# Third block's mixing: projection columns split in three equal banks, feature sums made as rows, last sums moved between halves of the output projection

## What is computed

```python
h = concatenate([meta, x], axis=1)              # 16 meta tokens ahead of 1024 tokens
u = rmsnorm_3(h, norm_mix_g)
x_lru, g_lru, v_cc, g_cc = split(u @ w_in)      # 4 x 512 features
xc = causal_depthwise_conv_3(x_lru, lru_conv_w, lru_conv_b)            # 4 taps
y_lru = rg_lru(xc, ...) * gelu(g_lru)           # gates, then a scan over the tokens
c = causal_depthwise_conv_3(v_cc * sigmoid(g_cc), cc_conv_w, cc_conv_b)  # 31 taps
y_cc = silu(layernorm_3(c, cc_ln_g, cc_ln_b))
y = concatenate([rmsnorm_3(y_lru, out_norm_lru_g), rmsnorm_3(y_cc, out_norm_cc_g)])
h = h + y @ w_out
h = h + square(relu(rmsnorm_3(h, norm_mlp_g) @ w_mlp_up)) @ w_mlp_down
return rmsnorm_3(h, norm_final_g)[:, 16:]
```

## Time and profile before

| | us |
|---|---|
| median of 3 runs (3903.34 to 3906.10) | 3903.86 |
| the profiled execution | 3905.99 |
| its span in the trace | 3904.1 |
| from the first full projection of the third block to the last matmul of out_3b (in the trace) | 2720.3 to 3142.2 |

### The profile page before, as it was taken

How to read it: one execution, slowest core, us unless ns; L and a number is a source line. 1 busy time by engine, 2 the same in 40 slices (tenths; PEclk the granted TensorE clock), 3 DMA queues, 4 the chain that set the end, 5 groups by cost and what they waited for, 6 DMA issues and landing times.

```text
span 3904.1 us, 38123 instructions
## 1 busy us (share of the span) xinstructions
PE 3515.0 (90%) x15786; PEld 2801.9 (72%) x15786; DVE 1294.2 (33%) x1735; ACT 714.9 (18%) x1060; POOL 1205.7 (31%) x1052
## 2 busy tenths in 40 slices
PE   5958997779969999999899999994989979999997
PEld 4556765668847568787688888883777768888886
DVE  4154065022140440313311111125888252222223
ACT  2210144121121440101100000003323220000011
POOL 3201201315423023343334343431432234343431
PEclk9978998889979899999999999997987989999998
DMA  2100100101221001112111111111001001111111
GB/s 113 43 17 27 43 1 22 54 11 54 86 92 52 14 23 44 54 43 86 36 51 44 53 43 54 43 54 60 33 22 65 33 33 53 45 51 45 44 53 43
DMA packets 31638, 179.52 MB, mean 46 GB/s; under 512 B 3744, under 2 KB 4768, under 8 KB 14624
## 3 DMA queue, kind: packets, MB, share of 16 engines
q1 hardware_dynamic: 18864, 137.37, 10.2%
q10 hardware_dynamic: 12656, 40.42, 2.8%
HBM read 163.10 MB, written 14.68 MB: 46 GB/s over the span
## 4 chain that ended last, share of the span: by engine, by line
PE 84%; DVE 11%; ACT 3%; issue 2%; POOL 1%; DMA 0%; DVEq 0%; ACTq 0%; POOLq 0%
PE ps L374 45%; PE ps L403 15%; PE ps L429 4%; PE ps L1635 4%; PE ps L678 2%; PE ps L1726 1%; DVE xlo L335 1%; PE ps L1684 1%; PE ps L1298 1%; DVE c_out L2014 1%; PE ps L1314 1%; PE ps L297 1%; DVE n_sq L329 1%; PE ps L291 1%; PE ps L740 1%
## 5 line engine op out<-in xcount | busy, mean ns | idle before, releaser
L469 POOL TENSOR_TENSOR whi<-raw,par 128x512 fp32r<-128x512 f32 x131 | 145.8, 1113 | 2592.5 <-PE ps L374 1869.5
L473 POOL TENSOR_TENSOR wlo<-raw,whi 128x512 fp32r<-128x512 f32 x524 | 783.6, 1496 | 41.7
L374 PE MATMUL ps<-xhi,whi 128*128 128x512 f32 x2304 | 723.7, 396 | 52.0 <-DVE xlo L335 32.4
L374 PE MATMUL ps<-xlo,whi 128*128 128x512 f32 x2304 | 715.7, 392 | 0.0
L374 PE MATMUL ps<-xhi,wlo 128*128 128x512 f32 x2304 | 714.9, 392 | 0.0
L374 PEld LDWEIGHTS ps<-xhi,whi 128*128 128x128 f32 x2304 | 434.5, 190 | 160.8 <-issue 32.5
L374 PEld LDWEIGHTS ps<-xlo,whi 128*128 128x128 f32 x2304 | 437.0, 190 | 92.4
L374 PEld LDWEIGHTS ps<-xhi,wlo 128*128 128x128 f32 x2304 | 435.8, 189 | 91.9
L471 POOL CAST whi<-raw 128x512 fp32r<-128x512 f32 x393 | 297.8, 758 | 0.0
L1190 DVE TENSOR_TENSOR h<-h,ps 128x1024 f32<-128x1024 f32 x112 | 132.2, 1218 | 414.0 <-PE ps L403 414.0
L403 PE MATMUL ps<-hidden_lo,whi 128*128 128x512 f32 x864 | 269.2, 393 | 0.0
(11 more groups left out here) (423 smaller groups left out, 4170.6 us busy)
## 6 DMA issues: line engine op xcount, KB each, us to landing
raw<-stream SPq DMA_DIRECT2D x131, 1024.0 KB, 4.8
h_scr<-h ACTq DMA_DIRECT2D x2, 4096.0 KB, 12.2
x_in<-xT ACTq DMA_DIRECT2D x4, 1024.0 KB, 14.4
x_again<-xT ACTq DMA_DIRECT2D x4, 1024.0 KB, 8.7
h<-h_scr ACTq DMA_DIRECT2D x1, 4096.0 KB, 13.9
outT<-h ACTq DMA_DIRECT2D x8, 512.0 KB, 3.0
bias<-bias ACTq DMA_DIRECT2D x1, 2560.0 KB, 19.3
o_scr<-o_staged ACTq DMA_DIRECT2D x2, 1024.0 KB, 4.8
```

Source lines behind the costliest of these rows:

```text
L374: mm = nc.tensor.matmul(ps[:, c0 + c:c0 + c + width], w, x(k, a, width), start=(n == 0 and m == 0), stop=(n == len(ks) - 1 and m == 2))
L469: nc.gpsimd.tensor_tensor(WHI[:, r, t], RAW[:, r, t], one, ALU.mult).then_inc(hi_done, 1)
L473: ins = nc.gpsimd.tensor_tensor(WLO[:, r, t], RAW[:, r, t], WHI[:, r, t].bitcast(F32), ALU.subtract)
```

## The change

1. The meta columns stand ahead of the tokens in `XH3` and `XL3`, so that the 1040 columns are one run. The twelve outputs v, g and x pass them in three pieces of 348, 346 and 346 columns (`THIRDS`), a PSUM bank each. ScalarE's two copies are of 348 columns and of the other two banks (692).
2. Feature sums: the column of ones is the weight and the data moves (`row_sums`), 2 matmuls of 512 columns for 128x1024 elements. The sums come as a row on partition 0 (and 32, for the convolution output). ScalarE takes the root of a row, or copies the rows, into `ROWS3`, and PE turns a row into 8 columns (`columns`, 8 transposes), which VectorE then reads from PSUM.
3. Order: cc_sums 0 and 1 stand ahead of the columns and the spread of the recurrence's norm, cc_sums 2 between the two. cc_sums 3 stands behind half 2 (before: half 4), its columns within half 3 and the two spreads within half 4. `rms_columns` stands before the third tile of out_3b's output 1, the spread before output 2. ScalarE's `keep_half` and `square` calls follow this.

```diff
+            ROWS3 = at("rows_3", A + 83264, [64, T])
+            THIRDS = ((0, 348), (348, 346), (694, 346))
...
-            chunks = ((0, HALF), (HALF, HALF)) if name in ("g_0", "g_2") else ((0, HALF), (HALF, HALF), (T, META))
+
+            chunks = ((META, HALF), (META + HALF, HALF)) if name in ("g_0", "g_2") else THIRDS
             for k in range(KB):
                 if ready:
                     pe.wait_ge(*ready(k))
                 w_hi, w_lo = WHI[:, r, KB * o + k, :], WLO[:, r, KB * o + k, :]
                 for m, (w, x) in enumerate(((w_hi, x3hi), (w_hi, x3lo), (w_lo, x3hi))):
-                    for a, width in chunks:
-                        mm = nc.tensor.matmul(ps[:, c0 + a:c0 + a + width], w, x(k, a, width),
+                    for i, (a, width) in enumerate(chunks):
+                        mm = nc.tensor.matmul(ps[:, c0 + BANK * i:c0 + BANK * i + width], w, x(k, a, width),
                                               start=(k == 0 and m == 0), stop=(k == KB - 1 and m == 2))
-                        if o == k == m == a == 0 and slot > 0:
+                        if o == k == m == i == 0 and slot > 0:
...
-            def column_sums(x, c, first, end):
-
-                for j in range(NT):
-                    mm = nc.tensor.matmul(ps[:, c + j:c + j + 1], x[:, P * j:P * (j + 1)], par("ones", 0, 1),
-                                          start=first and j == 0, stop=end and j == NT - 1)
-                return mm
-
-            def squares(s, c, first):
+            def row_sums(s, c, b, *more):
+
                 pe.wait_ge(*L("m_sq", s + 1))
-                column_sums(SQ3[:, s % 2, :], c, first, s % 4 == 3).then_inc(S("m_sum"), 1)
+                for a in range(0, T, HALF):
+                    for row, x in ((0, SQ3[:, s % 2, :]),) + more:
+                        mm = nc.tensor.matmul(ps[row:row + 1, c + a:c + a + HALF], par("ones", 0, 1), x[:, a:a + HALF],
+                                              start=(b == 0), stop=(b == 3))
+                mm.then_inc(S("m_sum"), 1)
 
             def cc_sums(b):
                 pe.wait_ge(S("cc_conv"), (CCK - 1) * (b + 1))
-                column_sums(CCO[:, b, :], OTHER + 2 * BANK, b == 0, False)
-                squares(4 + b, OTHER + 2 * BANK + NT, False)
+                row_sums(4 + b, OTHER + 2 * BANK, b, (32, CCO[:, b, :]))
+
+            def columns(row, c):
+                for j in range(NT):
+                    mm = nc.tensor.transpose(ps[:, c + j:c + j + 1], ROWS3[row:row + 1, P * j:P * (j + 1)],
+                                             IDENT[row:row + 1, row:row + 1])
+                return mm
...
             for b in range(4):
-                squares(b, OTHER + 3 * BANK, b == 0)
+                row_sums(b, OTHER, b)
+            cc_sums(0)
+            cc_sums(1)
+            pe.wait_ge(*L("l_root", 1))
+            columns(0, OTHER).then_inc(S("l_cols"), 1)
+            cc_sums(2)
             pe.wait_ge(*L("l_diag", 1))
             spread(DIAG3, OTHER).then_inc(S("l_inv"), 1)
-            for b in range(3):
-                cc_sums(b)
 
...
+            def cc_columns():
+                pe.wait_ge(*L("cc_rows", 2))
+                columns(32, OTHER)
+                columns(0, OTHER + BANK).then_inc(S("cc_cols"), 1)
+
+            def cc_spreads():
+                pe.wait_ge(*L("cc_diag", 2))
+                spread(DIAG3, OTHER).then_inc(S("cc_spread"), 1)
+                spread(DIAG3M, OTHER + 2 * BANK).then_inc(S("cc_spread"), 1)
+
+            for o in range(3):
                 lru_half(o)
             cc_sums(3)
-            lru_half(5)
-            pe.wait_ge(*L("cc_diag", 2))
-            spread(DIAG3, OTHER).then_inc(S("cc_spread"), 1)
-            spread(DIAG3M, OTHER + 2 * BANK).then_inc(S("cc_spread"), 1)
-            lru_half(6)
-            lru_half(7)
+            lru_half(3, (2, cc_columns))
+            lru_half(4, (1, cc_spreads))
+            for o in range(5, 8):
+                lru_half(o)
             pe.wait_ge(*L("lh_kept", 8))
...
-                    squares(8 + b, OTHER + 2 * BANK, b == 0)
+                    row_sums(8 + b, OTHER, b)
+
+            def rms_columns():
+                pe.wait_ge(*L("cc_rroot", 1))
+                columns(0, OTHER + 2 * BANK).then_inc(S("r_cols"), 1)
 
             def rms_spread():
                 pe.wait_ge(*L("cc_rdiag", 1))
-                spread(DIAG3, OTHER).then_inc(S("cc_inv"), 1)
+                spread(DIAG3, OTHER + 2 * BANK).then_inc(S("cc_inv"), 1)
 
             feature_tiles(pe, WH["out_3b"], 8, range(4, 8), xhi, xlo, ready=lambda n: L("cc_lo", n + 1),
-                          before={(1, 0): rms_sums, (1, 3): rms_spread, (2, 0): lambda: pe.wait_ge(*L("cc_inv_kept", 1))})
+                          before={(1, 0): rms_sums, (1, 2): rms_columns, (2, 0): rms_spread, (3, 0): lambda: pe.wait_ge(*L("cc_inv_kept", 1))})
...
-                nc.scalar.activation(dst[:, pad + META:pad + LW], trio(q), func).then_inc(free(q), 1)
-                nc.scalar.activation(dst[:, pad:pad + META], trio(q, T, META), func).then_inc(free(q), 1)
+                c, w, rest = 3 * BANK * (q % 2), THIRDS[0][1], THIRDS[1][1]
+                nc.scalar.activation(dst[:, pad:pad + w], ps[:, c:c + w], func).then_inc(free(q), 1)
+                nc.scalar.activation(dst[:, pad + w:pad + LW].rearrange("p (i t) -> p i t", i=2),
+                                     ps[:, c + BANK:c + 3 * BANK].rearrange("p (i t) -> p i t", i=2)[:, :, 0:rest], func)\
+                    .then_inc(free(q), 1)
...
-            nc.scalar.activation(LCOL[:, :], ps[:, OTHER + 3 * BANK:OTHER + 3 * BANK + NT], ACT.Sqrt, bias=EPSC,
-                                 scale=1.0 / (4 * P)).then_inc(S("l_root"), 1)
+            nc.scalar.activation(ROWS3[0:1, :], ps[0:1, OTHER:OTHER + T], ACT.Sqrt, bias=EPSC[0:1, :], scale=1.0 / (4 * P))\
+                .then_inc(S("l_root"), 1)
...
+            for o in range(2):
                 keep_half(o)
             act.wait_ge(S("cc_conv"), 4 * (CCK - 1))
             square(7, CCO[:, 3, :])
+            keep_half(2)
+            act.wait_ge(*L("m_sum", 8))
+            for row in (32, 0):
+                nc.scalar.activation(ROWS3[row:row + 1, :], ps[row:row + 1, OTHER + 2 * BANK:OTHER + 2 * BANK + T], ACT.Copy)\
+                    .then_inc(S("cc_rows"), 1)
             act.wait_ge(*L("cc_var", 4))
             nc.scalar.activation(RCOL[:, :], VCOL[:, :], ACT.Sqrt, bias=EPSC).then_inc(S("cc_root"), 1)
-            keep_half(5)
+            keep_half(3)
+            keep_half(4)
             for b in range(4):
                 act.wait_ge(*L("cc_moved", 2 * (b + 1)))
                 nc.scalar.activation(CCO[:, b, :], CCO[:, b, :], ACT.Silu, bias=par("cc_ln_b_3", b),
@@ -1924,15 +1957,15 @@
                 act.wait_ge(S("cc_silu"), b + 1)
                 nc.scalar.activation(XHI[:, 4 + b, :], CCO[:, b, :], ACT.Copy, scale=par("out_norm_cc_g_3", b))\
                     .then_inc(S("cc_hi"), 1)
-                if b < 2:
-                    keep_half(6 + b)
+                if b < 3:
+                    keep_half(5 + b)
...
-            dve.wait_ge(*L("l_root", 1))
-            v.step(nc.vector.reciprocal(LCOL[:, :], LCOL[:, :]))
+            dve.wait_ge(*L("l_cols", 1))
+            v.step(nc.vector.reciprocal(LCOL[:, :], ps[:, OTHER:OTHER + NT]))
...
-            s1, s2 = (ps[:, OTHER + 2 * BANK + NT * n:OTHER + 2 * BANK + NT * (n + 1)] for n in range(2))
-            dve.wait_ge(*L("m_sum", 8))
+            s1, s2 = (ps[:, OTHER + BANK * n:OTHER + BANK * n + NT] for n in range(2))
+            dve.wait_ge(*L("cc_cols", 1))```

PE, first projection output of the block (v0), before and after. `xhi3` and `xlo3` are the high and low parts of the normed input, `whi` and `wlo` those of the weights:

```order
L1635 MATMUL ps<-xhi3_291,whi_50 128x512 x2
L1635 MATMUL ps<-xhi3_291,whi_50 128x16
L1635 MATMUL ps<-xlo3_292,whi_50 128x512 x2
L1635 MATMUL ps<-xlo3_292,whi_50 128x16
L1635 MATMUL ps<-xhi3_291,wlo_51 128x512 x2
L1635 MATMUL ps<-xhi3_291,wlo_51 128x16
```

24 lines of the change are left out of this document (13 added, 11 removed).

## The result

| | before | after |
|---|---|---|
| median of the timed runs, us | 3903.78 (3903.34 to 3906.10) | 3865.69 (3863.78 to 3867.60) |
| span of the profiled execution | 3904.1 | 3865.1 |
| mean granted clock | 0.936 | 0.942 |
| first full projection of the block, to the end of out_3b | 2720.31 to 3142.19 = 421.88 | 2720.86 to 3103.38 = 382.52 |

A forecast was written before the change was run, and what follows sets the result against it. The kernel was taken as a line of PE work (84% of the chain); 18.9 + 1.2 + 7.8 - 1.2 + 3.7 = 30.4 us saved, and 3905.99 - 30.4 - 2.1 gave a forecast of 3874, range 3866 to 3897.

The forecast's parts named there:

- half 0 at half clock: Half 0, behind the last low part: a tile and the identity take 6.2 us, against 3.1 warm; end at 2995.7.
- the stall of 7.06: VectorE's wait for g1 at the second short convolution, 7.06 us, would go, making the lead 9.5.
- the one before the last scan: VectorE's wait of 6.06 us for an unchanged gelu output would stay, so the last scan has lead 18.9.
- the 7.95: VectorE's stall of 7.95 us before the third short convolution: some 5 would remain, at lead 14.2.
- rival 1: Row sums stay at half clock; half 0 ends at 3015.2, total 3897 us; chance 0.14.
- the walk: Warm step-by-step reckoning from first square at 2954.4 through four blocks (6.9 us) to the diagonal's end at 2975.0.
- a loss of 3.8: At the diagonal, 3.8 us of lead lost because cc_sums 0 and 1 stand ahead of the transposes; lead 15.1.
- the wait of 4.99: VectorE's wait of 4.99 us before its first low part would go, giving the low parts lead 20.1.
- Rival 4: Better case: half 0 warm and PE's restarts after gates shorter, total 3868 us; chance 0.05.
- rival 2: VectorE becomes the bound as GpSimd's splits fall beside its taps; costs some 8 us of 19, total 3882; chance 0.16.
- my signs of being wrong: Sums running at clock 0.50, taps slower than 1.47 us in the mean, or pieces of 347 taking over 0.2.
- The slower rival: An fp32r matmul of 347 columns is no shorter than one of 512 (0.2275 or more); total 3917 us; chance 0.05.

The follow-up runs named there:

- e1_pieces: The kernel before with only the twelve outputs' pieces changed to 348, 346 and 346 columns; 3884.12 us, ratio 0.9945.
- e9_same_row: The changed kernel with the convolution output's sums accumulated on the same output partition 0 as those of its squares; 3870.92 us, ratio 0.9912.
- e4: The changed kernel with the old pieces and the sums, transposes and spreads at the old places, so row sums without the new order; 3891.62 us, ratio 0.9964.
- e7: The changed kernel with ScalarE's sigmoids of features 1 and 2 ahead of its first product of the long convolution; 3864.57 us, ratio 0.9897.
- e3: The changed kernel with both matmuls of the squares first, then both of the convolution output, instead of alternating; 3865.84 us, ratio 0.9904.

## Why the prediction was right in kind and short in size

The direction and the course are as predicted; the sum was 30.4 us and is 39.4. Two steps failed: the price of the new sums and transposes (each matmul behind the other, 3.44 us a block of cc_sums, and 1.7 us for 8 transposes, where the runs show 1.80 and 0.65), and half 0 at half clock (6.2 us behind the last low part, where it took 3.4). At half 0 and among the halves behind it they are 6.5 of the 9.0 us by which the sum is short; 1.3 more came from the pieces, 0.7 on the way to the low parts and 0.5 in out_3b. Term by term, from the traces ("lead" is how much earlier a step comes; 0.55 us is added since the stretch begins that much later after):

| step | before | after | lead | predicted | term, measured | term, predicted |
|---|---|---|---|---|---|---|
| last scan's first step starts | 2954.17 | 2934.53 | 20.2 | 18.9 | 20.2 | 18.9 |
| last low part ends | 3009.7 | 2988.1 | 22.1 | 20.1 | 1.9 | 1.2 |
| half 0 ends | 3023.6 | 2991.5 | 32.6 | 27.9 | 10.5 | 7.8 |
| out_3b starts | 3084.30 | 3049.64 | 35.2 | 26.7 | 2.6 | -1.2 |
| out_3b ends | 3142.19 | 3103.38 | 39.4 | 30.4 | 4.2 | 3.7 |

- **Pieces: right.** A tile takes 0.474 us for 0.478. The line drawn between 0.119 at 256 columns and 0.2325 at 512 held within 1%. The reasoning on how much arrives held too: the stall of 7.06 is gone and the one before the last scan is left (4.32 of 6.06), with 20.2 us at the end where 18.9 were reckoned; of the 7.95 only 1.99 is left, for the 5 that I expected; e1_pieces gives 20.2 for this part by itself. The Trainium skill ("TensorE: Matmul & The Clock Gate", Back-to-back issue gap) would have made a tile 0.441 by its formula for an isolated matmul; the trace does not bear that out.
- **Clock of row sums: right.** 1.00, so rival 1 (0.14) did not come about. In the first four sums it was 0.82, where PE came to them from a wait of 2.89, and they took 8.50 us for the 6.9 of the walk. The rival's argument that every stretch of sums was at 0.50 rested on one window; in the kernel before, the sums in out_3b had 0.80. Its walk, by its own terms, ends with the diagonal at 2988.4, not 2990.
- **cc_sums and transposes: mis-sized.** I took each matmul one after the other (3.44 a block) and a transpose like a matmul of a column sum. A block takes 1.80 us and a transpose 0.08; e9_same_row, where all go to one partition, has the 3.5 a block that I had reckoned. VectorE's new wait for the columns is 2.39 instead of 5. At the diagonal that turned a loss of 3.8 into 0.8: it ends at 2971.25, a lead of 19.4 instead of 15.1. Only a part of these 4.3 us reached the low parts (22.1 for 20.1): the wait of 4.99 went as forecast, but the last three low parts now lie beside GpSimd's splits and take 2.3 us longer. Among the halves it is 1.6 for cc_sums 3 and 2.5 for 16 transposes (3.4 less the 0.9 by which they hold up half 3); the terms 2.6 and -1.2 lie 3.8 apart. This was the largest miss. The error was to add up the matmuls of cc_sums as if one had to end before the next, to price a transpose by a column sum at half clock, and to give neither term a lower end.
- **Half 0: mis-sized.** It ends 3.4 us behind the last low part, not 6.2. I reasoned that PE, having idled and stuttered, would be at half clock. It was, but only until 2985: PE passed the first two tiles at 0.50 to 0.64, with waits of 0.17 and 0.20 us behind them, and the windows show 1.00 again from 2985.9, before the last two. Rival 4 (0.05) named just this.
- **out_3b: right** within 0.5 us (5.85 and 6.96 against 5.5 and 6.9), as long as the order is changed too (e4).
- **VectorE as the bound (rival 2): half right.** Taps take 1.496 us in the mean instead of 1.470, about 3 us on 120, and VectorE does bound the middle of the projections (e7). Taps slower than 1.470 were one of my signs of being wrong, and that sign came. The stretch was shorter than forecast all the same; what the slower taps cost of it, no run tells apart.
- The slower rival did not come about; a piece of 347 takes 0.158.

What stays open: why matmuls overlap in the records that don't alternate in the program (e3), whether the place in PSUM or the partition decides (e9), and why half 0 came back to full clock when it did. The forecast lay 8.3 us too high, and errors the other way hid part of what it missed: the first squares took 1.6 us longer than reckoned and the low parts 2.3.

## What to carry to other kernels

Sum over partitions with the ones as the weight and the data moving: here few wide matmuls ran at 2.4 GHz (all but the first four blocks, behind a wait), where many one-column matmuls fell to 1.2, and a row is turned back into columns for 0.65 us. Where two such sums are wanted, put them on output partitions 0 and 32, and they cost as much as one (3.60 us for two blocks against 7.03 in e9, which shares its place in PSUM as well). When PE gets faster, look for the tail that its work had covered and start that tail earlier; and compare kernels by the length of the changed stretch, which came out the same within 0.1 us in two profiles, where single runs lie up to 8 us apart.
